# Finer filler in two causal attentions, gates by tanh, rope heads placed by ScalarE, memory transposes inside output stages

## The reference, cut to what matters

```
oa = (softmax(s1) - lam * softmax(s2)) @ va      # "diff", 4 heads, then a norm per head -> ya
ob = softmax(qb kb^T/8 + forget) @ vb            # "fox", 8 heads -> yb
merged = sigmoid(ga) * (ya @ w_diff_out) + sigmoid(gb) * (yb @ w_fox_out)
x = x + merged @ w_o
x = x + cross_attention(norm(x), norm(mem));  x = x + mlp(norm(x))
```

## Time and profile before

| what | value |
|---|---|
| median of 3 runs | 2545.98 us (2545.47 to 2546.41) |
| the profiled execution | 2548.65 us |
| its span, first to last instruction | 2546.7 us |
| PE busy / DVE / ACT / POOL | 95% / 51% / 37% / 40% |
| chain of work that ended last | PE 85%, DVE 10%, ACT 3%, issue 2% |
| mean granted TensorE clock | 0.981 |

### The profile page before, as it was taken

How to read it: one execution, slowest core, us unless ns; L and a number is a source line. 1 busy time by engine, 2 the same in 40 slices (tenths; PEclk the granted TensorE clock), 3 DMA queues, 4 the chain that set the end, 5 groups by cost and what they waited for, 6 DMA issues and landing times.

```text
span 2546.7 us, 30028 instructions
## 1 busy us (share of the span) xinstructions
PE 2430.2 (95%) x11158; PEld 1922.3 (75%) x11158; DVE 1286.5 (51%) x2121; ACT 951.6 (37%) x1424; POOL 1007.5 (40%) x744
## 2 busy tenths in 40 slices
PE   7998999999999999897999999999889999999998
PEld 6775667886888887665868888887556887888887
DVE  4454544414333335695436555556765424555555
ACT  4343344434322224622534222225656434322223
POOL 3331224332444444462524545444120241544443
PEclk9998999999999999898999999999999999999999
DMA  5221122331332222231312322332101431222331
GB/s 163 81 67 35 50 66 83 116 124 43 120 99 89 92 99 99 67 99 34 108 59 75 111 88 94 99 100 72 43 17 58 131 110 50 84 99 99 99 99 66
DMA packets 175562, 215.72 MB, mean 85 GB/s; under 512 B 6432, under 2 KB 157522, under 8 KB 175446
## 3 DMA queue, kind: packets, MB, share of 16 engines
q1 hardware_dynamic: 175446, 214.16, 26.0%
HBM read 212.04 MB, written 2.11 MB: 84 GB/s over the span
## 4 chain that ended last, share of the span: by engine, by line
PE 85%; DVE 10%; ACT 3%; issue 2%; DMA 0%; POOL 0%; DVEq 0%; SPq 0%; ACTq 0%
PE ps_l L761 74%; DVE arena L2296 3%; PE ps_l L972 3%; PE ps_l L1103 2%; PE ps_l L881 1%; PE ps_s L1035 1%; PE ps_s L1086 1%; ACT w_hi L1294 1%; DVE arena L1832 1%; DVE a_lo L1838 1%; DVE arena L2502 1%; DVE small L2519 0%; PE ps_s L987 0%; PE ps_s L851 0%; DVE x_T L2136 0%
## 5 line engine op out<-in xcount | busy, mean ns | idle before, releaser
L612 POOL TENSOR_TENSOR w_lo<-w_raw,w_hi 128x512 fp32r<-128x512 f32 (+1 forms) x740 | 1007.3, 1392 | 1512.9 <-ACT w_hi L1294 1501.1
L761 PE MATMUL ps_l<-a_hi,w_hi 128*128 128x512 f32 x1936 | 765.8, 396 | 22.1 <-DVE b_lo L2154 8.1
L761 PE MATMUL ps_l<-a_lo,w_hi 128*128 128x512 f32 x1952 | 762.8, 391 | 0.0
L761 PE MATMUL ps_l<-a_hi,w_lo 128*128 128x512 f32 x1936 | 757.6, 391 | 0.0
L1294 ACT ACTIVATE w_hi<-w_raw 128x2048 fp32r<-128x2048 f32 x197 | 372.3, 1890 | 600.5 <-PE ps_l L761 586.8
L761 PEld LDWEIGHTS ps_l<-a_hi,w_hi 128*128 128x128 f32 x1936 | 365.7, 189 | 107.0 <-issue 10.4
L761 PEld LDWEIGHTS ps_l<-a_lo,w_hi 128*128 128x128 f32 x1952 | 368.8, 189 | 79.5 <-issue 2.9
L761 PEld LDWEIGHTS ps_l<-a_hi,w_lo 128*128 128x128 f32 x1936 | 365.5, 189 | 77.8
L761 PE MATMUL ps_l<-b_hi,w_hi 128*128 128x512 f32 (+1 forms) x908 | 338.2, 373 | 21.0 <-DVE b_lo L2154 9.6
L761 PE MATMUL ps_l<-b_lo,w_hi 128*128 128x512 f32 (+1 forms) x908 | 335.7, 370 | 0.0
L761 PE MATMUL ps_l<-b_hi,w_lo 128*128 128x512 f32 (+1 forms) x908 | 335.6, 370 | 0.0
(11 more groups left out here) (273 smaller groups left out, 2662.8 us busy)
## 6 DMA issues: line engine op xcount, KB each, us to landing
w_raw<-in_ffn_w_up_dram SPq DMA_DIRECT2D x44, 1024.0 KB, 5.1
w_raw<-in_w_dram SPq DMA_DIRECT2D x32, 1024.0 KB, 5.2
w_raw<-in_ffn_w_down_dram SPq DMA_DIRECT2D x22, 1024.0 KB, 4.9
w_raw<-in_w_in_dram SPq DMA_DIRECT2D x20, 1024.0 KB, 5.4
w_raw<-in_xa_wkv_dram SPq DMA_DIRECT2D x16, 1024.0 KB, 5.6
w_raw<-in_w_kv_mem_dram SPq DMA_DIRECT2D x8, 1024.0 KB, 5.7
w_raw<-in_xa_wq_dram SPq DMA_DIRECT2D x8, 1024.0 KB, 5.1
w_raw<-in_xa_wo_dram SPq DMA_DIRECT2D x8, 1024.0 KB, 5.2
```

What stands on the lines that cost most here:

```text
L612: e.tensor_tensor(w_lo[:, b % 2, o], w_raw[:, b % 2, o], w_hi[:, b % 2, o].bitcast(F32), ALU.subtract).then_inc(w_lo_made[by], 1)
L761: ins = pe.matmul(o, *((v, w) if swap else (w, v)), start=first and n == 0, stop=last and n == 2)
```

## The change

- **Filler.** A group may be made in two halves of its contraction (`parts` 2: k = 0 to 3, then 4 to 7), in different steps. Its bank is claimed at the first half. The lag of diff goes from 1 to 2. The last `v_b` groups stand in steps 16 to 19. Fox starts with two `gate_a` groups in steps 0 and 1, `proj_a` follows from step 2, and the eight groups of `gate_b` are filler of steps 21 to 35. No product is added or removed.
- **Gates.** sigmoid(g) = (1 + tanh(g/2)) / 2: ACT makes tanh (`gate_tanh`) after the T copies, DVE uses (tanh + 1) * y in one operation (L2094, L2113 in the new numbering), and the factor 1/2 goes into the `A_hi` and `A_lo` copies. `merged` by gate a is made as filler (`fox_filled`).
- **Projection of fox.** `proj_b` is one stage of two blocks. In it, DVE's `A_lo` of a group follows directly on the next group's sum. The first block takes k outermost and claims all four banks at its start. The weight copies `hi` of the first two `w_o` blocks stand in the loop of the `A_hi` copies.
- **Memory.** `mem_turn(0)` and `mem_turn(2)` stand between the two halves of `w_o` and of `mla_o`, and the splitting on ACT and DVE stands with them.
- **Rope.** DVE adds all 128 rows at once, and ACT copies the four heads' 32 rows each into `qh`.

```diff
+        if (step, "P") in due:
+            ev.append(("P", due[step, "P"], 0))
         for item in fill.get(step, ()):
             ev.append(("G", item, 0))
-        for kind in "PVOMN":
-            if (step, kind) in due and (kind in "PVO" or "M" in extra):
+        for kind in "VOMN":
...
+    def feat_around(name, src, cols, between):
+        feat(name, src, "v", cols[0:2])
+        L.add(between, "vvvv")
+        feat(name + "+", src, "v", cols[2:4])
+        p.block_base[name + "+"] = p.block_base[name] + 2
...
+                fill.setdefault(step, []).append((tag, *divmod(n, parts), parts))
...
-    attention("diff", DIFF_HEADS, 1, "v", 2, extra="M", after=(1, 1, 0, 3, 4), fills=(
-        ("qk_b", "w_in", 8, 256, [(0, c) for c in (1536, 1792, 2048, 2304)], 2, "v", list(range(8))),
-        ("v_b", "w_in", 8, 256, [(0, c) for c in (2560, 2816)], 4, "a", [8, 9, 10, 11, 12, 14, 16, 18])))
-    def gates(tag, col, out):
-        for half in (0, 1):
-            feat(f"gate_{tag}{half}", "w_in", "v", [col + 512 * half, col + 512 * half + 256])
-            feat(f"proj_{tag}{half}", out, "v", [512 * half], nk=4, width=512)
+    attention("diff", DIFF_HEADS, 2, "v", 2, extra="M", after=(1, 1, 0, 3, 4), fills=(
+        ("qk_b", "w_in", 8, 256, [(0, c) for c in (1536, 1792, 2048, 2304)], 2, "v",
+         [0, 0, 1, 2, 3, 3, 5, 6, 7, 7, 8, 8, 9, 10, 11, 11], 2),
+        ("v_b", "w_in", 8, 256, [(0, c) for c in (2560, 2816)], 4, "a", [12, 13, 14, 15, 16, 17, 18, 19], 1)))
     attention("fox", FOX_HEADS, 3, "v", 1, extra="K", after=(2, 2, 3), fills=(
-        ("proj_a", "w_diff_out", 4, 512, [(0, 0), (0, 512)], 4, "a", [1, 2, 3, 4, 5, 6, 7, 7]),
-        ("gate_a", "w_in", 8, 256, [(0, 3080 + c) for c in (0, 256, 512, 768)], 2, "v",
-         [10, 12, 15, 18, 20, 23, 26, 30])))
-    gates("b", 4104, "w_fox_out")
-    feat("w_o", "w_o", "v", [0, 256, 512, 768])
+        ("gate_a", "w_in", 8, 256, [(0, 3080)], 2, "v", [0, 0, 1, 1], 2),
+        ("proj_a", "w_diff_out", 4, 512, [(0, 0), (0, 512)], 4, "a", [2, 2, 3, 3, 5, 6, 7, 7], 1),
+        ("gate_a+", "w_in", 8, 256, [(0, 3080 + c) for c in (256, 512, 768)], 2, "v",
+         [9, 9, 10, 11, 13, 13, 14, 15, 17, 17, 18, 19], 2),
+        ("gate_b", "w_in", 8, 256, [(0, 4104 + c) for c in (0, 256, 512, 768)], 2, "v",
+         [21, 21, 22, 23, 25, 25, 26, 27, 29, 29, 30, 31, 33, 33, 34, 35], 2)))
+    feat("proj_b", "w_fox_out", "v", [0, 512], nk=4, width=512)
+    feat_around("w_o", "w_o", [0, 256, 512, 768], "memT0")
     def keys(c, wkv):
         feat(f"xk{c}", wkv, "a", [0, 256, 512, 768], low_by="pppp" if c == 1 else "ppvv")
...
+            load_range(4, BB["proj_b"] + 2)
             wait_group(sp, L, plan.events["fox"][1]["V", FOX_HEADS - 1, 0])
             load_mem(0)
-            load_range(BB["proj_b0"], BB["mlp"] + 3)
+            load_range(BB["proj_b"] + 2, BB["mlp"] + 3)
...
+                        if not ks or 0 in ks:
+                            claim(pe, L, g + j, i, dg)
+                        for k in ks or range(nk):
...
+                                 ks=range(nk * part // parts, nk * (part + 1) // parts))
...
+            stage("proj_b", xb, nk=4, c=512, nb=2,
+                  ready=lambda k: wait_read(pe, L, plan.events["fox"][1]["V", 2 * k + 1, 0]))
...
+            stage("w_o", xa, nb=2, ready=lambda k: pe.wait_ge(m_lo, k + 1))
+            mem_turn(0)
+            stage("w_o+", xa, nb=2)
...
-            stage("mla_o", xa, ready=mo_ready)
+            stage("mla_o", xa, nb=2, ready=mo_ready)
+            mem_turn(2)
+            stage("mla_o+", xa, nb=2)
...
+                    if between and j == nb // 2:
+                        between()
+                        g = L.base[name + "+"] - KD // 2
...
+            def gate_tanh(n):
+                wait_read(act, L, gate_pos[n])
+                act.activation(gate(n % KD), gate(n % KD), ACT.Tanh, scale=0.5).then_inc(sg_r, 1)
...
+                    while gated < filled:
+                        gate_tanh(gated)
+                        gated += 1
...
+            while gated < 2 * KD:
+                gate_tanh(gated)
+                gated += 1
             mem_rstd(0)
-            gate_sigmoids("b", 1)
-            act.wait_ge(l_full, L.base["gate_b1"] + 4)
+            act.wait_ge(l_full, plan.fill_pos["gate_b"][KD - 1] + 1)
             for n in range(KD):
                 act.wait_ge(m_ready, n + 1)
-                act.activation(A_hi[:, n, :], merged[:, n, :], ACT.Copy).then_inc(m_hi, 1)
-            squares_and_z("w_o", 4, 1)
+                act.activation(A_hi[:, n, :], merged[:, n, :], ACT.Copy, scale=0.5).then_inc(m_hi, 1)
+                if n % 4 == 3:
+                    hi(plan.block_base["proj_b"] + n // 4 + 2)
...
-                    if half:
-                        act.wait_ge(rope_q, j + 1)
                     act.activation(rsh[:, 2 * j, :], bank(L, g + 2)[:, :], ACT.Copy).then_inc(l_free["a"], 1)
                     hi(plan.block_base[f"uq{half}{j}"] + 2)
                     if not half and not j:
                         latent_rstd()
+                for j in (0, 1):
+                    act.wait_ge(rope_v, 2 * half + j + 1)
+                    for e in range(4):
+                        ins = act.activation(qh[64:96, 4 * j + e, :], rsh[32 * e:32 * e + 32, 2 * j, :], ACT.Copy)
+                    ins.then_inc(rope_q, 1)
                 if not half:
...
+            def fox_filled(g, tag, n):
+                if tag == "gate_b":
+                    dve.wait_ge(sg_r, n + 1)
+                    wait_read(dve, L, plan.fill_pos["proj_a"][n])
+                    step(dve.scalar_tensor_tensor(out=merged[:, n, :], in0=gate(n), scalar=1.0, in1=merged[:, n, :],
+                                                  op0=ALU.add, op1=ALU.mult))
+                    sync()
+                scaled(g, 1, lambda j: gate(n + 2 if tag == "gate_a+" else n))
...
+            def merged_low(n):
+                dve.wait_ge(m_hi, n + 1)
+                dve.scalar_tensor_tensor(out=A_lo[:, n, :], in0=merged[:, n, :], scalar=0.5,
+                                         in1=A_hi[:, n, :].bitcast(F32), op0=ALU.mult, op1=ALU.subtract)\
+                    .then_inc(m_lo, 1)
...
+                g = L.base["proj_b"] + n
+                wait_group(dve, L, g)
+                dve.wait_ge(sg_r, KD + n + 1)
+                dve.scalar_tensor_tensor(out=s_buf[:, n % 4, :], in0=gate(n), scalar=1.0, in1=bank(L, g)[:, :],
+                                         op0=ALU.add, op1=ALU.mult).then_inc(l_free["v"], 1)
+                wait_read(dve, L, g)
+                dve.tensor_tensor(merged[:, n, :], merged[:, n, :], s_buf[:, n % 4, :], ALU.add)\
+                    .then_inc(m_ready, 1)
+                if n:
+                    merged_low(n - 1)
+            merged_low(KD - 1)
...
+                        if n == KD // 2:
+                            between()
+                        if n >= KD // 2:
+                            g = g0 + 4
...
                     wait_read(dve, L, L.base[f"uq{half}{j}"] + 2)
-                    if half:
-                        dve.wait_ge(rope_q, 2 + j)
+                    dve.wait_ge(rope_v, 2 * half + j)
                     v, turned = rsh[:, 2 * j, :], rsh[:, 2 * j + 1, :]
                     turn_half(v, turned, slice(0, P))
-                    for e in range(4):
-                        q = slice(32 * e, 32 * e + 32)
-                        ins = dve.tensor_tensor(qh[64:96, 4 * j + e, :], v[q, :], turned[q, :], ALU.add)
-                    ins.then_inc(rope_q, 1)
+                    dve.tensor_tensor(v, v, turned, ALU.add).then_inc(rope_v, 1)
```

More of the change, by code:

```diff
@@ L1 @@
 from contextlib import ExitStack
+import itertools
 import numpy as np
@@ L170, in attention @@
         fill = {}
-        for tag, _, _, _, places, per, _, steps in fills:
-            assert len(steps) == per * len(places)
+        for tag, _, _, _, places, per, _, steps, parts in fills:
+            assert len(steps) == per * len(places) * parts
             for n, step in enumerate(steps):
-                fill.setdefault(step, []).append((tag, n))
+                fill.setdefault(step, []).append((tag, *divmod(n, parts), parts))
         ev = attention_events(heads, lag, extra, after, fill)
@@ L193, in attention @@
             elif kind == "G":
[L194 to L195 removed]
+                tag, _, part, parts = h
+                if part == parts - 1:
+                    p.fill_pos.setdefault(tag, []).append(len(L.who))
+                    L.who += [next(who for t, *_, who, _, _ in fills if t == tag)]
             elif kind in "OPN":
@@ L198, in attention @@
         p.events[name] = (ev, at)
-        for tag, src, nk, width, places, per, _, _ in fills:
+        for tag, src, nk, width, places, per, _, _, parts in fills:
             p.block_base[tag] = len(p.blocks)
-            p.fill_pos[tag] = [at["G", (tag, n), 0] for n in range(per * len(places))]
```

(17 more changed lines are left out.)

108 lines of the change are left out of this document (39 added, 69 removed).

## The result

The changed kernel takes **2516.8 us** (median, 2515.3 to 2517.6) against 2545.7 before: a ratio of 0.988, 95% interval 0.9868 to 0.9892. The forecast was 2509, with a range of 2501 to 2524. The direction and the range held; 8 us of the 37 did not come.

What follows compares the result with a forecast made beforehand. PE, busy for 95% of the span, was taken as the bound, so only its idle or slow-clock time could be won. The terms summed to -37.3 us, from 2545.98 to a forecast of 2509 us, range 2501 to 2524.

Steps and rivals of the forecast that it cites:

- Part a: End of diff and start of fox: five PE waits, 13.05 us, and lost clock are won back; -19 us.
- Part b: End of fox: two PE waits for the copy of a transpose go, covered by half gate groups; -1.6 us.
- Part c: Last V to `w_o`: wait for `A_lo` and low clock go, a new 1.4 us wait at `proj_b` comes; -5 us.
- Part d: Memory transposes in `w_o` and `mla_o`: the wait behind them only shortens, 0.9 us less each; -1 us for both.
- The margins: `proj_b` to `w_o`: `A_lo` and the second block's piece come 1 to 2 us before wanted; 1 us counted lost.
- Part e: Rope at the two starts of mla: shorter DVE sums remove or shorten PE's waits and low clock; -12.5 us.
- Part f: Switching between stretches of filler on PE costs 0.1 us each; gates on ACT cost nothing; +1.8 us.
- Diff half filled: Rival at the end of diff: waits across DVE and low clock partly stay, -10 in place of -19, 2518 us; chance 0.12.
- DVE against POOL in `proj_b`: Rival: two-SBUF-operand DVE operations and POOL exclude one another, PE loses 10 us more, 2519 us; chance 0.15.
- Rope to ACT: Rival in rope: the wait moves from DVE to ACT, -5 in place of -12.5, 2516 us; chance 0.10.
- The banks: Rival in diff and fox: half groups hold banks, PE waits 0.87 us in 53 steps, 2555 us; chance 0.04.
- That the change does nothing: Rival for the whole kernel: moved work was already covered, waits return one stage later, 2545 us; chance 0.03.

Runs made afterwards that it cites:

- experiment 6: Changed kernel with diff's lag back at 1: 2518.3 us; with diff's old whole-group filler steps, lag 2 kept: 2518.9 us; with both: 2528.6 us.
- Experiment 7: Changed kernel with whole filler groups in place of halves, each in the step of its first half, in diff and fox: 2520.1 us.
- experiment 1: Changed kernel with the memory transposes again behind the four blocks of `w_o` and of `mla_o`, all else as changed: 2510.5 us.
- experiment 8: Changed kernel with its 16 gates by Sigmoid in place of tanh, adding table loads on ACT inside fox: 2517.0 us.

## Why the prediction was right, and where it was wrong

Against the profiled executions, with idle time and clock by the table above:

- **Part a, -19 forecast.** Idle 13.05 to 0.54, clock 8.3 to 0: -20.8. Right, and nearly at its bound of -21; the 2 us kept back for DVE being late were not needed. The mechanism as told was too simple: lag and filler were both named as covers, each with a share of the waits, and experiment 6 shows that either covers nearly all four waits in diff (1.5 and 2.1 us are lost with one gone, 11.8 with both).
- **Part b, -1.6.** The waits of 0.87 and 0.78 us are gone: -1.65. Experiment 7 shows that halves do more than this term says.
- **Part c, -5.** The wait of 4.16 became one of 1.78: -2.4. The clock's 3.4 did not come in the changed kernel, because the moved transposes put a low stretch into the same `w_o`; in experiment 1 it came, 3.0 us. By the two traces that makes -5.4, so the term is right, and what spoiled it is part d. No run has part c alone. The margins held without the 1 us: `w_o` never waits for `A_lo`. DVE's first `A_lo` came 13.6 us after the last V, the forecast's number, but not for its reason: DVE waited 9.48 us for PE's first block there, and `mem_rstd` held up nothing.
- **Part d, -1, bounds -3 and +2: the step that failed.** "It only shortens", by 0.9 each, was right to 0.1: 4.8 to 4.0. But the price of the other side, "`xk`'s second weight block loses the 6.7 us of rest", was named and then counted as next to nothing, and the clock was not in the term at all. Measured by experiment 1: **+6.3**. By stretch, the changed kernel less experiment 1 (profiled executions, 7.0 us apart): +2.0 in `w_o` (clock +2.9, idle -0.8), +1.7 from `xk0` to 1700 (none of it in `xk0` itself; 1.5 is the low stretch near 1195, far from part d, and its cause is open), +0.8 in `mla_o` (clock +1.6, idle -0.8), +2.8 behind `xk2` (idle +2.6). It was not the second block that paid, which waits for POOL by 0.27 us, but the fourth, whose load is late and which DVE splits: 2.29. This term was off by 7.3 us, and the forecast missed by 7.8.
- **Part e, -12.5.** -11.3 in the trace, -11.5 alone. The value groups of `uk1` no longer wait, those of `uk0` wait 0.87 (0.7 forecast), and the weights of `uk1` come 0.86 earlier (0.7). The 0.8 us counted for ACT's longer work came too: PE's first scores wait 1.65 where it was 0.98. That the sum is so near is in part luck. The stretch won 8.4 us of idle time, where the terms said 7.0, but only 2.3 us of clock, where they said 6.8: two low stretches of 3.41 us are left, behind the waits for ACT and for POOL's low part. Before and after:

```profile
1805.91 0.46 PE L1035 MATMUL ps_s<-arena 96*128 96x128 f32 x2 [0.98 <-ACT arena L1765]
...
1875.43 0.50 PE L761 MATMUL ps_l<-b_hi,w_hi 128*128 128x512 f32 x1 [2.89 <-POOL w_lo L612]
```
```profile
1777.09 0.46 PE L1040 MATMUL ps_s<-arena 96*128 96x128 f32 x2 [1.65 <-ACT arena L1785]
...
1846.11 0.52 PE L771 MATMUL ps_l<-b_hi,w_hi 128*128 128x512 f32 x1 [2.03 <-POOL w_lo L622]
```
- **Part f, +1.8.** The time that is neither idle nor clock grew by 0.9 us up to `w_o`. Gates on ACT cost nothing (experiment 8), as said.

So the forecast held because its large terms came out right in sum: without part d it says -36.3, and experiment 1 measured -35.8. Parts a and c gave 2.2 us more than forecast and parts e and f 2.1 less, which nearly cancels.

**The rivals.** Diff half filled: no. DVE against POOL in `proj_b` (0.15): the premise was wrong, not the rule. DVE's operations there, changed kernel, and the only POOL block that falls into them:

```profile
399.12 0.69 DVE L2105 SCALAR_TENSOR_TENSOR a_lo<-arena,a_hi 128x512 fp32r<-128x512 f32 x1
...
401.60 1.78 DVE L2105 SCALAR_TENSOR_TENSOR a_lo<-arena,a_hi 128x512 fp32r<-128x512 f32 x1
...
405.00 1.78 DVE L2105 SCALAR_TENSOR_TENSOR a_lo<-arena,a_hi 128x512 fp32r<-128x512 f32 x1
```
```profile
399.82 6.41 POOL L622 TENSOR_TENSOR w_lo<-w_raw,w_hi 128x512 fp32r<-128x512 f32 x4 [15.27 <-ACT w_hi L1306]
```

Operations of two SBUF operands take 0.69 us until POOL starts at 399.8, and up to 1.78 beside it. That a DVE instruction with two SBUF inputs contends with a GpSimd instruction that reads SBUF is the rule of the Trainium skill ("SBUF — State Buffer", section Who interferes with whom), and this trace agrees. But POOL had been idle for 15 us, and only four of the 16 were met: 3.1 us of DVE's time, none of PE's. Rope to ACT: no, ACT's eight copies (5.1 us) cost PE only the 0.67 us more ahead of its first scores. The banks: no wait over 0.6 us in diff or fox; half a group holding a bank for a step costs nothing here. That the change does nothing: no.
